# The modulation's sums over partitions: from matmuls with a column of ones to 32x32 turns on VectorE and a 128x32 table on TensorE

## The reference, cut to what matters

```python
cond = jax.nn.silu(c)                                          # [1, 1024]
mod = (cond @ ada_w[layer] + ada_b[layer])[:, None, :]         # first block: 6 x 1024 columns a layer
sh1, sc1, g1, sh2, sc2, g2 = jnp.split(mod, 6, axis=-1)
h = rms_norm(x, norm_mix_g[layer]) * (1.0 + sc1) + sh1
...
ml = jnp.split((jax.nn.silu(c) @ w_ada[i] + b_ada[i])[:, None, :], N_MOD, axis=-1)   # second block: 9 x 1024
mc = jnp.split(jax.nn.silu(c_ctx) @ w_ada[i] + b_ada[i], N_MOD, axis=-1)             # and a second condition
```

## Time and profile before

| | us |
|---|---|
| median of three runs | 3001.05 (2995.84 to 3003.23) |
| span of the profiled execution | 3001.2 |
| PE busy in it | 2880.9 |
| DVE busy in it | 1824.3 |
| ACT busy in it | 1153.6 |

### The profile page before, as it was taken

How to read it: one execution, slowest core, us unless ns; L and a number is a source line. 1 busy time by engine, 2 the same in 40 slices (tenths; PEclk the granted TensorE clock), 3 DMA queues, 4 the chain that set the end, 5 groups by cost and what they waited for, 6 DMA issues and landing times.

```text
span 3001.2 us, 42837 instructions
## 1 busy us (share of the span) xinstructions
PE 2880.9 (96%) x17454; PEld 2493.1 (83%) x17454; DVE 1824.3 (61%) x2924; ACT 1153.6 (38%) x1649; POOL 0.2 (0%) x4
## 2 busy tenths in 40 slices
PE   6999999989999999899999999999999999998999
PEld 5889998879998766688888867888888888897999
DVE  4657778655556556577576555654556745566655
ACT  3345443443434444432222344422223222245544
POOL 0000000000000000000000000000000000000000
PEclk9999999979999999899999999999999999999999
DMA  9738766467767778455463221353534546532564
GB/s 312 257 118 239 231 207 215 134 168 207 232 176 279 303 268 303 144 168 189 116 189 120 60 85 43 113 161 92 146 121 134 184 122 178 165 81 78 157 187 135
DMA packets 557035, 511.41 MB, mean 170 GB/s; under 512 B 14308, under 2 KB 533543, under 8 KB 556711
## 3 DMA queue, kind: packets, MB, share of 16 engines
q1 hardware_dynamic: 477350, 390.56, 42.1%
q10 hardware_dynamic: 79488, 118.11, 12.3%
HBM read 507.57 MB, written 1.05 MB: 169 GB/s over the span
## 4 chain that ended last, share of the span: by engine, by line
PE 85%; DVE 6%; ACT 3%; DMA 3%; issue 2%; SPq 1%; ACTq 0%; DVEq 0%
PE bank L762 24%; PE bank L763 23%; PE bank L764 23%; PE bank L1081 3%; DMA weights_raw<-in_moe_w 2%; PE bank L974 2%; DVE ring L2184 1%; DVE hn_split L2190 1%; PE bank L1030 1%; PE bank L790 1%; PE bank L1032 1%; PE bank L1031 1%; DVE weights_split L2131 1%; ACT weights_split L1609 1%; DVE weights_split L2360 1%
## 5 line engine op out<-in xcount | busy, mean ns | idle before, releaser
L762 PE MATMUL bank<-hn_split,weights_split 128*128 128x256 f32 (+1 forms) x3096 | 1029.6, 333 | 43.9 <-DVE weights_split L2131 19.0
L763 PE MATMUL bank<-hn_split,weights_split 128*128 128x256 f32 (+1 forms) x3096 | 1012.1, 327 | 0.0
L764 PE MATMUL bank<-hn_split,weights_split 128*128 128x256 f32 (+1 forms) x3096 | 1011.8, 327 | 0.0
L2131 DVE TENSOR_TENSOR weights_split<-weights_raw,weights_split 128x1024 fp32r<-128x1024 f32 (+2 forms) x520 | 673.2, 1295 | 229.8 <-ACT weights_split L1609 228.8
L1609 ACT ACTIVATE weights_split<-weights_raw 128x1024 fp32r<-128x1024 f32 (+2 forms) x520 | 577.6, 1112 | 562.2 <-PE bank L764 522.3
L762 PEld LDWEIGHTS bank<-hn_split,weights_split 128*128 128x128 f32 x3096 | 600.1, 194 | 114.8 <-issue 47.0
L763 PEld LDWEIGHTS bank<-hn_split,weights_split 128*128 128x128 f32 x3096 | 600.7, 194 | 47.1 <-issue 1.9
L764 PEld LDWEIGHTS bank<-hn_split,weights_split 128*128 128x128 f32 x3096 | 600.1, 194 | 46.8
L762 PE MATMUL bank<-hidden_split,weights_split 128*128 128x256 f32 (+1 forms) x1177 | 388.4, 330 | 0.0
L764 PE MATMUL bank<-hidden_split,weights_split 128*128 128x256 f32 (+1 forms) x1177 | 385.7, 328 | 0.0
L763 PE MATMUL bank<-hidden_split,weights_split 128*128 128x256 f32 (+1 forms) x1177 | 385.6, 328 | 0.0
(11 more groups left out here) (415 smaller groups left out, 2794.5 us busy)
## 6 DMA issues: line engine op xcount, KB each, us to landing
weights_raw<-in_w_ffn_in SPq DMA_DIRECT2D x176, 512.0 KB, 5.2
ada_halves<-in_w_ada ACTq DMA_DIRECT2D x96, 768.0 KB, 4.8
weights_raw<-in_moe_w SPq DMA_DIRECT2D x80, 704.0 KB, 6.7
ada_halves<-in_ada_w ACTq DMA_DIRECT2D x54, 768.0 KB, 4.8
weights_raw<-in_moe_w SPq DMA_DIRECT2D x66, 512.0 KB, 5.4
weights_raw<-in_w_in SPq DMA_DIRECT2D x60, 512.0 KB, 5.5
expert_down<-in_moe_w SPq DMA_DIRECT2D x25, 1024.0 KB, 5.6
weights_raw<-in_w_ffn_out SPq DMA_DIRECT2D x32, 768.0 KB, 4.8
```

The source lines that it names most:

```text
L762: mm(ps, wh, xh, start=first, stop=False)
L763: mm(ps, wh, xl, start=False, stop=False)
L764: return mm(ps, wl, xh, start=False, stop=last)
L2131: tt(split_view(slot, 1, kts, n), raw, split_view(slot, 0, kts, n).bitcast(F32), ALU.subtract)\
```

## The change

It replaces the third step, the sum over partitions, and adds a table `fold` of 128x32 that has a one at row s and column s % 32.

- In the nets and in layer 1's mixer, when a chunk's sums are done, DVE turns the 128x384 in 32x32 blocks (`turn_sums`), which leaves 32 of the 128 rows' values side by side in each partition, and adds these 32 (`add_parts`, a reduction to 12 columns for each condition). What remains is four groups of 32 partitions to be added. `ada_fold` does that once for a whole turn, not for each chunk: four matmuls with `fold` as weights, one for each 32 partitions of the result. `turn_sums` stands in front of the split of unit p+2, `add_parts` behind it.
- At the start and in the mixture of experts DVE turns PE's rows in 32x32 blocks out of the bank, in place of ACT's copy, and `fold_rows` adds the quarters with the same table: four matmuls in place of four (start) or three (experts).
- The eleven chunks of layer 0's mixer keep their copy by ACT and `ada_columns`.
- ACT's loads of `ada_halves` are no longer behind its copies. The quarters of the sums in the nets come a little earlier (24 units in place of 25).

```diff
-                self.sum_at = [2 + 25 * q // (4 * self.per) for q in range(4 * self.per)]
+                self.sum_at = [2 + 24 * q // (4 * self.per) for q in range(4 * self.per)]
+                self.parts = FOLD1 if self.first_block else FOLD2
+                self.fold_at = 36 if name == "in1.1" else 28
...
+            def fold_rows(place, rows, tiles, conds, bank=4):
+                view = rows[:, 0:tiles * P].rearrange("p (t m j) -> p t m j", m=4, j=32)
+                for m in range(4):
+                    i = mm(PS[bank][32 * m:32 * m + 32, place:place + conds * tiles], tab("fold"), view[:, :, m, 0:conds],
+                           start=True, stop=True)
+                i.then_inc(ada_done, 1)
...
-            def ada_sums(g, x, p):
-                for c in range(x.per):
-                    if p == x.sum_at[4 * c + 3] + 2:
...
-                        for t in range(ADA_TILES):
-                            for s in range(x.conds_of(g, c)):
-                                at_col = x.conds * (ADA_TILES * c + t) + s
-                                i = mm(PS[4][:, at_col:at_col + 1], x.sums[c % 2][s][:, t * P:(t + 1) * P], tab("ones")[:, 0:1],
-                                       start=True, stop=True)
-                        i.then_inc(ada_done, 1)
+            def ada_fold(g, x, p):
+                if p == x.fold_at:
+                    pe.wait_ge(mod_ready, g + x.mods)
+                    pe.wait_ge(ada_folded, x.folded(g, x.per - 1))
+                    n = x.conds * ADA_TILES * x.per
+                    for m in range(4):
+                        i = mm(PS[4][32 * m:32 * m + 32, 0:n], tab("fold"),
+                               x.parts[:, m, :, :].rearrange("p t s -> p (t s)")[:, 0:n], start=True, stop=True)
+                    i.then_inc(ada_done, 1)
...
-                    for n in range(4):
-                        act.wait_ge(first_rows, n + 1)
-                        if n >= 2:
-                            act.wait_ge(ada_done, n - 1)
-                        act.activation(ROWF[n % 2][:, :], PS[(7, 0)[n % 2]][:, :], ACT.Copy).then_inc(first_copied, 1)
...
+            def turn_sums(g, x, p):
+                for c in range(x.per):
+                    if p == x.sum_at[4 * c + 3] + 1:
...
+                        for s in range(conds):
+                            i = dve.transpose(x.turned[s].rearrange("p t m j -> p (t m j)"), x.sums[c % 2][s][:, :])
+                        i.then_inc(ada_turned, 1)
+
+            def add_parts(g, x, p):
+                for c in range(x.per):
+                    if p == x.sum_at[4 * c + 3] + 1:
...
+                        for s in range(conds):
+                            i = dve.reduce_sum(x.parts[:, :, 3 * c:3 * c + 3, s].rearrange("p m t -> p t m"), x.turned[s][:, :, :, :], AX.X)
+                        i.then_inc(ada_folded, 1)
...
+                def turn_rows(n):
+                    dve.wait_ge(ada_used, x.halves(n, 0, 1) + 2)
+                    dve.wait_ge(ada_done, x.done(n - 1))
+                    dve.transpose(AROW[:, :], PS[7][:, 0:ADA_COLS]).then_inc(ada_copied, 1)
...
+            for n in range(4):
+                dve.wait_ge(first_rows, n + 1)
+                if n >= 2:
+                    dve.wait_ge(ada_done, n - 1)
+                dve.transpose(ROWF[n % 2][:, :], PS[(7, 0)[n % 2]][:, :]).then_inc(first_copied, 1)
```

More of the change, by code:

```diff
@@ L61 @@
           ("ret_decay", 512), ("ret_key", 4), ("ret_query", 256), ("restart", 512), ("causal", 64),
-          ("inv_freq", 1), ("eps", 1), ("iota", 8), ("adapick", 2), ("tokpick", 15)]
+          ("inv_freq", 1), ("eps", 1), ("iota", 8), ("adapick", 2), ("tokpick", 15), ("fold", 32)]
 TABLE_AT = {}
@@ L114, in tables @@
     t["tokpick"][:, 7] = 1.0
+    t["fold"][s, s % 32] = 1.0
     for j in range(4):
@@ L443, in program, with __init__ @@
         class AdaTurns:
-            def __init__(self, name, chunks, tiles, mods, first):
+            def __init__(self, name, chunks, tiles, mods, first, dones, folds):
                 turns, _, self.n = FFN[name] if name in FFN else (1, SEQ, 24)
@@ L480, in halves, with folded, done @@
                 return g * (2 * self.per) + (2 * (self.chunks + c) + h + 1)
-            def done(self, g, c):
-                return g * self.per + (4 + self.chunks + c + 1)
+            def folded(self, g, c):
+                return self.folds + g * self.per + c + 1
+            def done(self, g):
+                return self.dones + g + 1
         in_view = a["ada_w"][0][:, 15 * P:48 * P].rearrange("(h k p) (c n) -> c h p k n", p=P, k=4, n=ADA_COLS)
-        ADA, _chunks, _tiles, _mods, _first = {}, IN_CHUNKS, 48, 2, 0
+        ADA, _chunks, _tiles, _mods, _first, _dones, _folds = {}, IN_CHUNKS, 48, 2, 0, 4 + IN_CHUNKS, 0
         for _n in ("ffn1.0", "in1.1", "ffn1.1", "ffna.0", "ffnb.0", "ffna.1"):
-            x = ADA[_n] = AdaTurns(_n, _chunks, _tiles, _mods, _first)
+            x = ADA[_n] = AdaTurns(_n, _chunks, _tiles, _mods, _first, _dones, _folds)
+            _dones += x.n_turns
+            _folds += 0 if _n == MOE else x.n_turns * x.per
             _chunks += x.n_turns * x.per
@@ L1798, in experts @@
                     for v in range(3, UP_UNITS):
-                        if v == 11 and b == 0:
-                            copy_ada(7)
                         split_up(UP_UNITS * b + v)
@@ L2491, in experts @@
                     for v in range(3, UP_UNITS):
+                        if v == 11 and b == 0:
+                            turn_rows(7)
                         split_up(UP_UNITS * b + v)
```

75 lines of the change are left out of this document (47 added, 28 removed).

## The result

Median 2953.16 us (2952.36 to 2957.56, four runs), against 3001.18 us (2995.84 to 3003.23, four runs) for the kernel before: ratio 0.9852, 95% interval 0.9838 to 0.9865, which is 40.5 to 48.6 us. The prediction said 43.1 us, and 2958 us in a range of 2944 to 2976.

The account below looks back on a forecast made before the run. It took TensorE to bound the nets, with VectorE having room. Removed matmuls -52.3, folds +3.2, experts -1.6, mixer +3.5 and start +4.1 sum to -43.1 us, so 3001.05 becomes 2958 us, range 2944 to 2976.

Parts of the forecast that it names:

- The removed matmuls: In the nets, 468 one-column records leave TensorE, 1.34 us per two-condition chunk and 0.67 per one-condition chunk: -52.3 us.
- The folds: Eight folds in the nets, four new matmuls each, cost TensorE 0.4 us apiece: +3.2 us (0.8 to 7.8).
- The experts: In the dense experts, six groups of records at 0.67 us become folds at 0.4: -1.6 us.
- VectorE's price: On VectorE, each chunk and condition takes a 128x384 transpose and a reduction, 0.55 us each.
- Cover in the nets: In the nets, VectorE's new work fits into its waits for TensorE, so it costs 0.
- Both places at which it could break: Nets: slack before a split (3.6 us in `ffna.0`, 1.1 in `ffn1.0`), and VectorE's wait per pair (0.9 to spare).
- Layer 1's mixer: Five of eight chunks put 1.1 us of VectorE work on the path, three gain 0.67: +3.5 us (0 to +8.8).
- The start: ACT's early `ada_halves` loads, 1.573 MB, run beside `ada_first` and the first weights: +4.1 us (0 to +6).
- both losses stay away: Rival: early loads use spare queue time and the mixer's additions fall into waits; 2950 us, chance 0.14.
- nothing freed: Rival: in the nets, removed matmul time returns as TensorE waits for splits; 3000 us, chance 0.03.
- The rival of a slower kernel: Rival: VectorE becomes the bound in the nets through dear transposes; 3015 us at x = 3.2, chance 0.03.
- its formula: Slower-kernel rival: 30 x (1.33x - 2.37) us lost in the nets, x being transpose and reduction together; 43 us at 2.85.

Follow-up runs that it names:

- all five mixers without turns: Layer 1 mixer on TensorE's column of ones: the kernel before, profiled twice, and the changed kernel with mixer undone (2948.96), plus late loads (2944.67), plus useless matmuls (2952.12 us).
- the three kernels that load late and have no filler: Changed kernel with early loads behind row banks (2949.70), behind ACT's first split (2949.04), or the latter plus column-of-ones mixer (2944.67 us); none has the 16 useless matmuls.
- the second profile of before: The kernel before, unchanged, measured and profiled once more beside the experiments: 2998.10 us, ratio 1.0004.

## Why the prediction was right

**The removed matmuls** (-52.3): put back, they cost 52.6 us in the nets. **The folds** (+0.4 each): 0.42 from the starts. **The experts** (-1.6): -1.67 by the means, 1.55 when undone. **VectorE's price** (0.55 and 0.55): 0.56 and 0.54. **Cover in the nets** (0): twice the transposes cost about 1 us in `ffn1.0` and nothing that shows elsewhere. Both places at which it could break were the right ones, and both broke with four times the transposes: VectorE's waits (0.9 us to spare a pair, or 1.35 for a chunk's three units, where the trace has 1.1) and the slack in front of a split (3.6 and 1.1 us).

**Layer 1's mixer** (+3.5): +2.3 against two profiles of before, 3.3 against all five mixers without turns. The count was not exact: six additions on the path instead of five, and 2.4 us of gains instead of 2.0. The sign named for it, TensorE's waits for VectorE longer by some 5 us, came.

**The start** (+4.1): +4.95. Its mechanism was right, bytes ahead of `ada_first`; moving the loads away gives 4.05, and TensorE's last rows then start 4.1 us earlier (32.70 for 36.81). The other 0.9 is not the loads'. In the three kernels that load late and have no filler these rows still start at 32.57 to 32.70, where the two profiles of before have 31.35 and 31.08; the cheaper folds win some of it back, and why the last piece lands later is open. That the rows take 3.6 us instead of 1.92 is no sufficient cause by itself: in the second profile of before they took 3.52, and its first split started at 36.98.

**The rivals.** That both losses stay away fell with the loads and the mixer; so did "nothing freed", with the matmuls put back. The rival of a slower kernel didn't come, since a transpose costs 0.56, but its mechanism is real. With four times the transposes, 2.6 us of transposes and reduction for a chunk and condition ((4.25 + 1.00)/2), its formula, from VectorE's total, gives 30 x (1.33 x 2.6 - 2.37) = 33; the two nets with those pairs lost 36.9. Its threshold, a loss of the whole gain only at 2.85, was too high all the same, since the nets lost 51 us in all: what it left out is the slack in front of one split, which cost 14.6 in the other two nets while VectorE had time to spare.

The sum of stages is -44.1, the prediction -43.1, the ratio says 40.5 to 48.6. The single profiled pair, 49.9 apart, would have asked for another cause for 6.8 us; 4.8 of it were the routed experts, which the second profile of before took away. That the start's 0.9 too little and the mixer's 1.2 too much nearly cancel in the sum is luck.

## What to carry to other kernels

A one-column matmul in float32 with 128x128 weights cost TensorE 0.11 us a record here, so a sum over partitions was better prepared on an engine with room and added once for many chunks. What moves to that engine is free while it fits two rooms, and both are to be read: the engine's idle time in the stretch where the work lands (not its average over the kernel), and the slack in front of the next thing that TensorE waits for. With four times the transposes the first was passed in two nets and the second in two others. And an edit that takes instructions out of a queue lets the loads behind them run earlier: look up what they then run beside.

## What the hardware showed that was not expected

- Records of 128x32 weights and 512 columns in float32 that go to four groups of 32 partitions in turn took 1.92 us for 16, 0.12 each; to one and the same group, 13.47 us for 31, 0.43 each. So the four groups worked side by side, and the first price doesn't hold for one of them alone.
- The granted clock was 0.50 in the 4 us around the rows that followed a wait of 4.85 us at the start, and 1.00 in the same stretch when the wait was filled; 16 records took 3.64 us behind that wait. But the same kernel before took 1.92 behind a wait of 0.89 in one profile, and 3.52 behind 0.98 in another, so the length of the wait alone doesn't tell.
- The routed experts took 319.3 to 327.3 us in profiles of kernels that do the same there, and before's layer 1 mixer 195.8 and 191.2, at a granted clock of 0.87 and 0.89: a difference of 5 us in a single pair of profiles, in a stage without an edit, was no effect.
